# Two transformer blocks on one core: TensorE takes over the pooling's means, VectorE the queries' rotation, scores move to other PSUM banks, and the mLSTM's queries and keys are worked in twelve blocks of 128 features

## The reference, cut to what matters

```python
def mlstm_mixer(u, ...):                       # first block, layer 1
    qk, v, o_pre, gates = split(u, [1536, 2304, 3072])
    qk = silu(causal_dwconv(qk, qk_conv_w))    # width 4, 1536 features
    q, k = split(qk, 2)                        # 4 heads of 192 features
    h = mlstm_chunkwise(q, k, v, log_i, log_f)
    h = (h - mean) * rsqrt(var + eps) * head_norm_g
    return sigmoid(o_pre) * h

def mixer_sublayer(h, ...):                    # second block
    u_pool, u_conv, c_q, c_kv, k_r, g_logits = split(h @ w_in, ...)
    gates = sigmoid(g_logits + b_gate)         # 3 x 1024 features
    y_pool = pool_mixer(u_pool) @ pool_proj    # 4 groups of 128 features
    y_conv = conv_module(u_conv) @ conv_proj   # a * sigmoid(gate), 31 taps,
                                               # layer norm, silu
    y_mla = mla(c_q, c_kv, k_r, ...) @ mla_proj  # 8 heads, 64 + 32 features,
                                               # the 32 are rotated
    return (gates[0]*y_pool + gates[1]*y_conv + gates[2]*y_mla) @ w_out

def pool_mixer(u, w_grp, scale):               # group g: window 2, 4, 8, 16
    mixed = mean of the last min(t + 1, window) tokens - u
    return (mixed @ w_grp[g]) * scale
```

## Time and profile before

| what | us |
|---|---|
| median of 3 runs (lowest, highest) | 1609.09 (1609.03, 1609.48) |
| the profiled execution's own time | 1608.99 |
| its span, from the first to the last instruction | 1607.2 |
| TensorE busy in the span | 1543.8 (96%) |
| VectorE busy | 1138.4 (71%) |
| ScalarE busy | 897.7 (56%) |
| GpSimd busy | 101.8 (6%) |
| mLSTM: first query pair to the end of the last | 721.5 to 783.3 |
| second block: end of the latents to the start of `mla_proj_2` | 1046 to 1217 |

### The profile page before, as it was taken

How to read it: one execution, slowest core, us unless ns; L and a number is a source line. 1 busy time by engine, 2 the same in 40 slices (tenths; PEclk the granted TensorE clock), 3 DMA queues, 4 the chain that set the end, 5 groups by cost and what they waited for, 6 DMA issues and landing times.

```text
span 1607.2 us, 22098 instructions
## 1 busy us (share of the span) xinstructions
PE 1543.8 (96%) x8926; PEld 1358.6 (85%) x8926; DVE 1138.4 (71%) x1628; ACT 897.7 (56%) x1356; POOL 101.8 (6%) x137
## 2 busy tenths in 40 slices
PE   7999999999999999999999999798999989999996
PEld 6888899888888888889978888797999778888885
DVE  5666666666667666655776566769867878989997
ACT  5455454455545555456545555444456657777774
POOL 0000000000000000001300000042002320000000
PEclk9999999999999999999999999899999999999998
DMA  9655454555555555343455554335334659999992
GB/s 359 211 191 197 159 196 162 195 218 197 186 183 198 196 183 191 138 148 101 160 207 222 189 197 162 133 125 210 131 106 164 234 210 350 354 347 345 359 368 103
DMA packets 48059, 332.99 MB, mean 207 GB/s; under 512 B 5712, under 2 KB 5840, under 8 KB 10192
## 3 DMA queue, kind: packets, MB, share of 16 engines
q1 hardware_dynamic: 46496, 321.43, 55.0%
q0 software_dynamic: 1456, 10.09, 1.6%
HBM read 330.45 MB, written 1.05 MB: 206 GB/s over the span
## 4 chain that ended last, share of the span: by engine, by line
PE 83%; DVE 10%; ACT 3%; POOL 1%; issue 1%; DMA 0%; SPq 0%; DVEq 0%; ACTq 0%; POOLq 0%
PE psw L505 54%; PE psy L505 28%; DVE wlo L1650 4%; DVE kT L2037 2%; PE psw L508 1%; ACT whi L1147 1%; POOL ar L2434 1%; DVE xs L1659 0%; DMA raw<-in_ws 0%; ACT xs L1147 0%; ACT ar L1147 0%; DVE x L1733 0%; POOL rstd L2354 0%; DVE gsel L2227 0%; DVE x L1746 0%
## 5 line engine op out<-in xcount | busy, mean ns | idle before, releaser
L1650 DVE TENSOR_TENSOR wlo<-raw,whi 128x1024 fp32r<-128x1024 f32 (+2 forms) x552 | 640.5, 1206 | 192.2 <-ACT whi L1147 186.7
L505 PE MATMUL psw<-xs,whi 128*128 128x512 f32 (+3 forms) x2544 | 687.3, 345 | 18.5 <-DVE wlo L1650 8.5
L1147 ACT ACTIVATE whi<-raw 128x1024 fp32r<-128x1024 f32 (+2 forms) x552 | 540.0, 1031 | 150.2 <-PE psy L505 107.0
L505 PE MATMUL psw<-xs,wlo 128*128 128x256 f32 (+2 forms) x1928 | 516.3, 282 | 2.1 <-DVE xs L1659 2.1
L505 PEld LDWEIGHTS psw<-xs,whi 128*128 128x128 f32 (+2 forms) x2544 | 427.4, 187 | 68.8 <-DVE wlo L1650 8.5
L505 PEld LDWEIGHTS psw<-xs,wlo 128*128 128x128 f32 (+2 forms) x1928 | 362.9, 188 | 17.4 <-issue 2.6
L505 PE MATMUL psw<-whi,xs 128*128 128x512 f32 (+1 forms) x704 | 178.9, 365 | 6.3 <-DVE xs L1659 5.1
L505 PE MATMUL psy<-whi,hhi 128*128 128x512 f32 x472 | 158.0, 390 | 0.0
L505 PE MATMUL psy<-whi,hlo 128*128 128x512 f32 x472 | 157.8, 389 | 0.0
L505 PE MATMUL psy<-wlo,hhi 128*128 128x512 f32 x472 | 157.7, 389 | 0.0
L505 PEld LDWEIGHTS psw<-whi,xs 128*128 128x128 f32 x704 | 126.0, 190 | 27.6 <-issue 2.6
(11 more groups left out here) (303 smaller groups left out, 1624.2 us busy)
## 6 DMA issues: line engine op xcount, KB each, us to landing
raw<-in_ws SPq DMA_DIRECT2D x252, 1024.0 KB, 4.8
ar<-in_ws SPq DMA_DIRECT2D x32, 1024.0 KB, 6.5
raw<-in_ws SPq DMA_DIRECT2D x17, 768.0 KB, 4.3
gb<-in_ln POOLq DMA_DIRECT2D x8, 1024.0 KB, 6.1
raw<-in_ws SPq DMA_DIRECT2D x4, 672.0 KB, 3.9
ar<-in_memT SPq DMA_DIRECT2D x2, 1024.0 KB, 13.7
ar<-in_xT SPq DMA_DIRECT2D x2, 512.0 KB, 5.4
raw<-in_ws SPq DMA_DIRECT2D x2, 512.0 KB, 6.3
```

Of the source, the lines that this page charges most:

```text
L505: return e.matmul(o, l, rr, start=start, stop=stop)
L1147: return e.activation(o, i, ACT.Copy, **k)
L1650: e.tensor_tensor(wlo[i % NS][:, c0:c1], raw_t[slot[i]][:, c0:c1], whi[i % NS][:, c0:c1].bitcast(f32), ALU.subtract).then_inc(*made.up((i, ...
```

## The change

- **mLSTM.** Queries and keys in 12 blocks of 128 features: three tiles of 256 columns for each of the two parts. Heads of 192 features now cross blocks, so `attend` takes 128 + 64 rows. The work between the tiles is dealt anew on six entries; `attend(2)` joins `attend(3)`, and `states(2)` joins `states(3)`, in the output gate.
- **Pooling.** The inputs are made token by row, in two tiles of 4 x 512 columns and 48 matmuls of 512. The means are a product with a constant matrix (`means`, 0.79 MB, a new input, loaded on GpSimd's queue into a buffer that the gates use later): eight f32 matmuls, 1,536 columns in all, between the two `uq` tiles. GpSimd's sums go. The groups' products stand behind gate half 1, in two banks.
- **Order.** `glu(0)` comes before the latents' transposes, the pooling's inputs after `glu(1)`. One gate half moves from behind `rstd` to ahead of the mean. The convolution's taps are dealt anew.
- **Rotation.** VectorE rotates the queries in six operations on 128x256; ScalarE spreads the keys.
- **Attention.** The scores use `psy` banks 6 and 7. ScalarE copies the turned queries and keys out ahead of the exponentials.
- **End.** ScalarE rounds the convolution's result before the sigmoids of a gate, and prepares one more tile there.

```diff
...
-    for h in range(4):
+    for j in range(3):
         for part in range(2):
-            n = 768 * part + 192 * h
-            tiles.append(("w_in_mlstm", (0,), 0, 8, n, n + 192))
+            n = 768 * part + 256 * j
+            tiles.append(("w_in_mlstm", (0,), 0, 8, n, n + 256))
...
-    for j in range(2):
-        tiles.append(("w_in_2", (0,), 0, 8, 256 * j, 256 * j + 256))
     for j in range(2):
         for part in range(2):
             n = 512 + 512 * part + 256 * j
             tiles.append(("w_in_2", (0,), 0, 8, n, n + 256))
+    rows("w_in_2", (0,), 8, 0, 512, 4)
...
+        means = mg[:, 0:4 * 384].rearrange("p (g n) -> p g n", g=4)
...
                 def attend(h):
-                    q_, k_ = qk[h % 2]
+                    rows = [(192 * h, 192 * h + 128), (192 * h + 128, 192 * h + 192)] if h % 2 == 0 else [
+                        (192 * h, 192 * h + 64), (192 * h + 64, 192 * h + 192)]
                     b = bank("attend", h)
                     for part in range(2):
-                        need.wait_ge(*act.at("qk", h, part))
-                    for f in range(2):
-                        mm(b[:, 0:256], k_[:, f, 0:128], q_[:, f, :], f == 0, f == 1)
-                    for f in range(2):
-                        ins = mm(b[:, 256:384], k_[:, f, 128:256], q_[:, f, 128:256], f == 0, f == 1)
+                        need.wait_ge(*act.at("qk", (192 * h + 191) // 256, part))
+                    at = [(qk[r0 // 256 % 2], r0 // 128 % 2, r0 % 128, (r1 - 1) % 128 + 1) for r0, r1 in rows]
+                    for f, ((q_, k_), blk, p0, p1) in enumerate(at):
+                        mm(b[:, 0:256], k_[p0:p1, blk, 0:128], q_[p0:p1, blk, :], f == 0, f == 1)
+                    for f, ((q_, k_), blk, p0, p1) in enumerate(at):
+                        ins = mm(b[:, 256:384], k_[p0:p1, blk, 128:256], q_[p0:p1, blk, 128:256], f == 0, f == 1)
...
-                for h in range(4):
+                steps = [lambda: (turn(1, 0), weights(0)), lambda: (value(1, 0), turn(1, 1), weights(1)),
+                         lambda: (attend(0), value(1, 1), turn(1, 2)), lambda: (states(0), value(1, 2), turn(1, 3), weights(2)),
+                         lambda: (attend(1), value(1, 3), weights(3)), lambda: (states(1), finish(1))]
+                for j in range(3):
                     for part in range(2):
-                        pair(("head", h, part), Tile("w_in_mlstm", 768 * part + 192 * h), xhi, xlo, x_rows(4), m=96)
+                        pair(("head", j, part), Tile("w_in_mlstm", 768 * part + 256 * j), xhi, xlo, x_rows(4))
...
-                         {0: lambda: attend(3), 1: lambda: states(3)})
+                         {0: lambda: (attend(2), attend(3)), 1: lambda: (states(2), states(3))})
...
+            glu(0)
...
+            glu(1)
+            rows_p = [bank("pool", t) for t in range(2)]
             for j in range(2):
-                pair(("glu", 0, j), Tile("w_in_2", 512 + 256 * j), xhi, xlo, x_rows(6))
-                pair(("glu", 1, j), Tile("w_in_2", 1024 + 256 * j), xhi, xlo, x_rows(6))
+                w = Tile("w_in_2", 0)
+                for t in range(2):
+                    done = ([("bank", ("pool", t))] if j else []) + ([w.used()] if t else [])
+                    rows_of(w, t, xhi, xlo, w.k0, [(rows_p[t][:, :], 0, 512)], j == 0, j == 1, x_rows(6), [done] if done else ())
+
+            def pool_means():
+
+                for i in range(2):
+                    b = bank("pooled", i)
+                    need.wait_ge(*act.at("up", 1))
+                    need.wait_ge(*means_in.at("means"))
+                    for f in range(2):
+                        g, c = 2 * i + f, 256 * f
+                        mm(b[:, c:c + 256], up_[:, 0, 128 * g:128 * g + 128], means[:, g, 0:256], True, False)
+                        ins = mm(b[:, c + 128:c + 256], up_[:, 1, 128 * g:128 * g + 128], means[:, g, 256:384], False, True)
+                    ins.then_inc(*pe.up(("bank", ("pooled", i))))
+
+            def pool_groups():
+                for i in range(2):
+                    b = bank("poolw", i)
+                    need.wait_ge(*act.at("pooled", i))
+                    for f in range(2):
+                        g = 2 * i + f
+                        ins = mm(b[:, 256 * f:256 * f + 256], P("pool_w", 128 * g, 128 * g + 128), pooled[:, g, :], True, True)
+                    ins.then_inc(*pe.up(("bank", ("poolw", i))))
...
+                if i == 0:
+                    pool_means()
...
-            for _ in range(4):
+            for n in range(8):
                 gate_half()
-            for g in range(4):
-                b = bank("poolw", g)
-                need.wait_ge(*pool.at("pooled", g))
-                ins = mm(b[:, 0:256], P("pool_w", 128 * g, 128 * g + 128), pooled[g][:, 16:272], True, True)
-                ins.then_inc(*pe.up(("bank", ("poolw", g))))
-            for _ in range(4):
-                gate_half()
+                if n == 1:
+                    pool_groups()
...
-                b = bank("scores", h)
+                b = claim(6 + i, "scores", h)
...
+            gate_half()
...
-            gate_half()
...
+                steps = [lambda: (turn(1, 0), weights(0)), lambda: (turn(1, 1), weights(1)), lambda: turn(1, 2),
+                         lambda: (states(0), turn(1, 3), weights(2)), lambda: weights(3), lambda: (states(1), finish(1))]
...
+            glu(1)
+            w.tile()
+            w.tile()
+            for t in range(2):
+                from_bank(("pool", t), up_[:, t, :], flat, ("up", t))
...
+                if i == 0:
+                    for n in range(2):
+                        from_bank(("pooled", n), pooled[:, 2 * n:2 * n + 2, :], lambda b: blocks(b[:, :], 256), ("pooled", n))
...
+                need.wait_ge(*dve.at("kr", t))
+                copy(kf[:, t, :, 64:96], kr[:, t, :].unsqueeze(1).to_broadcast([128, 8, 32])).then_inc(*act.up(("kf", t)))
...
-                for back, stage in ((3, turn_p), (1, scores), (0, turn_qk)):
+                for back, stage in ((3, turn_p), (0, turn_qk), (1, scores)):
...
-            gate_half()
+            need.wait_ge(*act.at("ca", 3))
+            copy(mhi[:, 4:8, :], ca).then_inc(*act.up(("convhi",)))
+            w.ahead(3)
...
                 steps = [lambda: None, lambda: None, lambda: attend(0), lambda: states(0), lambda: (attend(1), scale(1)),
-                         lambda: (states(1), finish(1)), lambda: attend(2), lambda: states(2)]
-                for h in range(4):
+                         lambda: (states(1), finish(1))]
...
-                w.rows(4, {0: lambda: attend(3), 1: lambda: states(3)})
+                w.rows(4, {0: lambda: (attend(2), attend(3)), 1: lambda: (states(2), states(3))})
...
+
+            w.tile()
+            w.tile()
+            glu(0)
+            for i, nb, g in ((0, 3, "q_g"), (1, 2, "kv_g")):
...
+            w.tile()
+            conv_some(5)
+            w.tile()
+            conv_some(5)
+            glu(1)
+            conv_some(4)
             for i in range(2):
                 w.tile()
-                conv_some(6)
+                conv_some(7)
+            for i in range(2):
+                w.tile()
+                conv_some(5)
             w.rows(1)
-            conv_some(6)
+            conv_some(2)
+            need.wait_ge(*act.at("qf", 1, 1))
+            x1, x2 = qf[:, :, :, 64:80], qf[:, :, :, 80:96]
+            cb_ = cosA.unsqueeze(2).to_broadcast([128, 2, 8, 16])
+            sb_ = sinA.unsqueeze(2).to_broadcast([128, 2, 8, 16])
+            for i, (a, c) in enumerate(((x1, cb_), (x2, sb_), (x2, cb_), (x1, sb_))):
+                ins = e.tensor_tensor(roped[:, i, :, :, :], a, c, ALU.mult)
+            then(ins)
...
-            for _ in range(4):
+            for n in range(8):
                 gate_half()
-                conv_some(5)
-            for g in range(4):
...
-            conv_some(4)
+                if n == 1:
+                    for g in range(4):
+                        rest(mlo[:, g, :], place["poolw", g // 2][:, 256 * (g % 2):256 * (g % 2) + 256], mhi[:, g, :], ("poolhi", g // 2),
+                             P("pool_scale", g, g + 1)).then_inc(*dve.up(("poolT", g), *([took(("poolw", g // 2))] if g % 2 else [])))
+                conv_some(3)
...
-                    conv_some(3)
+                    conv_some(2)
...
                     scores(step - 1)
+                conv_some(4 if 0 < step < 9 else 5)
                 gate_half()
-                conv_some(4)
-            conv_some(1000)
...
+            gate_half()
+            conv_some(1000)
...
+            e.dma_start(means, A["means"][:, :].rearrange("p (g n) -> p g n", g=4)).then_inc(*means_in.up(("means",)))
...
-            then(e.memset(up_[:, :, 0:16], 0.0))
-            need.wait_ge(*act.at("up", 1))
-            for g in range(4):
-                src, lo = up_[:, g, :], 0
-                bufs = [wsum[:, g, :], wt2[:, g, :]]
```

(26 more changed lines are left out.)

168 lines of the change are left out of this document (71 added, 97 removed).

## The result

The kernel after takes 1582.99 us (median of 4 runs, 1581.49 to 1584.22), the kernel before on the same chip 1609.28 (1609.03 to 1610.63). The ratio is 0.9832, with an interval of 0.9820 to 0.9844 (the quotient of the two medians, 0.9837, lies inside it): 26.3 us less, where the forecast had 29.3.

What follows compares the result with a forecast made beforehand. TensorE was taken to bound the kernel, busy 96% of the span, but VectorE the second block. Terms summed to -29.3: span 1607.2 to 1577.9, with 1.8 around it and 0.1 for the median 1579.8, said as 1580; range 1576 to 1585.

Steps and rivals of the forecast that it cites:

- The pairs (-10.4): mLSTM: six pairs of 48 matmuls at 5.75 us replace eight at 5.61, saving 10.4 us.
- loading sets the pace, the rival: mLSTM pairs: weight loading sets the pace, so wider blocks cost what fewer save; 10.4 us lost, 1590; chance 0.03.
- at the same price, no gain: mLSTM's end: `attend(2)` and `states(2)` move behind the pairs at an unchanged price; no gain.
- The first wait (-3.3): mLSTM, second pair: spreading `weights` removes a bank wait of 1.6 us and 1.7 lost to the clock; -3.3.
- The end of the mLSTM (+0.4): mLSTM's end: heads 2 and 3 reach GpSimd together, so the heads' transposes wait; +0.4 us.
- the rival of +3: mLSTM's end: GpSimd takes two heads in a row at the highest price; +3, 1583; counted within the forecast's 0.62.
- The second block, what goes (-10.1): Second block: `zc` ready early, no wait for `poolT`; 6.7 us idle, 2.2 of clock and 1.2 of waits go; -10.1.
- The attention (-8.2): Second block's attention: ScalarE copying first removes waits of 3.1 and twice 1.25 us and 2.6 of clock; -8.2.
- The means (+2.8): Second block, between `uq`'s tiles: the pooling means as f32 matmuls on TensorE add 2.8 us.
- the inputs by row (-0.6): Second block: pooling inputs made by row take 10.9 us for 11.5; -0.6.
- The end (0): End of the mixers: ScalarE's rounding first changes nothing; 0, at the best -1.3 us.
- The rival on the other side: Attention: small f32 products and short bank waits keep the clock low; up to 38 us more, 1618; chance 0.02.

Runs made afterwards that it cites:

- e3: Kernel after with only the order of `attend`'s four products changed, to 128, 64, 64, 128 rows: 1582.07 us, ratio 0.9827.
- e1: Kernel after with all four `weights` of the mLSTM back in step 0: 1585.44 us, ratio 0.9846.
- e5: Kernel after with one `weights` behind tile 2 of the values' rows, two behind tile 3, one in step 0: 1580.87 us, ratio 0.9817.
- e6: Kernel after with both the edit of e5 and the order of `attend`'s products from e3: 1578.50 us, ratio 0.9807.
- e8: Kernel before with one line moved, GpSimd's memset of `zc` ahead of its pooling sums: 1607.67 us, ratio 0.9984.
- e9: Kernel after with ScalarE's old attention order, exponentials ahead of the copy of the turned queries and keys: 1585.00 us, ratio 0.9842.
- e12: Kernel after with ScalarE's old order at the mixers' end, sigmoids ahead of the rounding, no tile prepared ahead: 1584.17 us, ratio 0.9835.
- e10: Kernel after with the attention's scores back on the banks handed out in turn: 1582.96 us, ratio 0.9827.
- e2: Kernel after with all exponentials of `weights` ahead of the first silu, two of the four `weights` in step 0: 1584.86 us, ratio 0.9844.
- e4: Kernel after with both the early `weights` of e2 and the order of `attend`'s products from e3: 1584.17 us, ratio 0.9838.
- e7: Kernel before with the mLSTM's part of the change alone: 1599.59 us, ratio 0.9935.
- e11: Kernel after with the rotation of the queries given back to GpSimd: 1580.17 us, ratio 0.9818.

## Why the prediction was right, and where it was off

The direction, the place and most of the size were right: 26.3 us of 29.3. A gave 4.6 us less than forecast and C 1.1 more, and B came out 0.7 shorter, which isn't the change's; that the whole is off by only 3 is in part luck. To see which terms failed I take all the work in A and in C by its starts in TensorE's timeline, each piece from its start to the next one's. By the forecast's own steps:

- **The pairs (-10.4).** Right, -10.8. A pair of 128 columns takes 5.86 us (721.74 to 727.60), and the six 35.1 without the waits for silu; the eight of before, at 5.73 where nothing disturbed them, 45.9. The forecast had both prices 0.1 too low (5.75 and 5.61), as it took too much off for the attention product between two pairs (1.42 us for 1.23); the two errors nearly cancel. That loading sets the pace, the rival, is out.
- **`attend`, "at the same price, no gain".** This is the step that failed most: the four take 7.6 us for 5.1, so +2.5 where the forecast had 0. It counted records and columns and took the earlier trace rows for the price, though the split of the contraction changed from 96 + 96 to 128 + 64 rows. e3 showed that the changes between them cost part of it: halving them gave 0.7 back.
- **The first wait (-3.3).** The wait and its clock went, but they were worth 2.3 and not 3.3. The forecast took 1.6 us of idle time from the earlier trace rows, which are waits of PEld, the weight loading. TensorE's own timeline of before has one wait of 1.00, in the row below. The low clock behind it cost 1.3 us by the length of the next pair, where the forecast had 1.7.

```profile
729.95 1.36 PE L505 MATMUL psw<-ar 4*128 4x256 f32 x4 [1.00 <-ACT ar L1147]
```

- **`weights` spread over the steps.** It was costed by its banks alone, with 0.1 for silu. Its price on ScalarE, six table loads, came back as two new waits for silu of 0.51 and 0.53 us, which make two pairs 1.35 longer (the third, of 0.30, was there before as 0.22). And the small products around it took 0.7 more. Most of that are the transposes and the memory's products, 9.4 us for 8.9 in A; in e1 and e5, where the `weights` stand together, they take 8.9 again. e5 took 1.6 us of A away.
- **The end of the mLSTM (+0.4).** Cheaper, 0: GpSimd was done at 797.0 and VectorE's products at 800.9, ahead of the transposes at 802.25; the rival of +3 is out.
- With these the 4.6 us missing in A are accounted for: 2.5 `attend`, 1.25 silu, 1.0 the first wait, 0.7 the small products, less 0.4 each for the pairs and the end. e6 gets 2.6 of them back.
- **The second block, what goes (-10.1).** From the start of C to the first transposes of the attention TensorE took 94.8 us before (1045.76 to 1140.53) and 87.0 after (1036.65 to 1123.62): -7.8, where the forecast with the means and the inputs had -7.9. There is no wait for `zc` or `poolT`. But the first reason given, that `zc` is there sooner, is worth 1.9 us by itself (e8); the count of VectorE's queue behind it carried the term. VectorE took `poolT` at 1095.03, after waiting 0.46 us for ScalarE's part of it, and about 5.4 us before gate half 4 began at 1100.5.
- **The attention (-8.2).** From there to `mla_proj_2` it is 76.4 us before and 67.0 after: -9.4, so the 1.1 us that C gained over the sum lie here. The three waits of before and the low clock behind them cost about 9.1 us by the lengths of the products there, not 8.2. No wait is left and no stretch below 1.00. ScalarE's order, undone alone, is about half of it (e9), and for two of the three waits it isn't shown to be the cause.
- **The means (+2.8), the inputs by row (-0.6).** The means took 2.5 us from start to start, the inputs 10.91 (1062.13 to 1073.04): right. A step took 4.91 us and not 5.1.
- **The end (0).** Right as a sum, 46.46 to 46.27. But it needs ScalarE's new order there: without the earlier rounding and the tile prepared with it, it is 2.7 us longer (e12).
- **The clock.** The rival on the other side is out: 1.00 over all the attention, with the scores' small f32 products between the halves. The Trainium skill's case (TensorE: Matmul & The Clock Gate, section on PSUM-queue cycling) was not met here.

## What to carry to other kernels

Before spreading small work over a loop, count its price on every engine, not only the resource that it frees: an exponential between two silus is two table loads, and a step has room for as many banks as are empty by then. An early start helps an engine only if its queue can use it, so look for the point where the queue is full; ahead of that point idle time costs nothing. When a wait is to be priced, read it in the row of the engine that does the work: TensorE's own wait was 1.00 us where its weight loading showed 1.6. And compare traces by stretches between common starts: e10 and e12 were "the same" by their whole time and 1.9 and 2.7 us slower where they differed.

## What the runs showed of the hardware

- **Table loads.** A load took 1.28 us each time. The Trainium skill (ScalarE: Activation LUTs, section What ACT_TABLE_LOAD costs) gives the same 1.28 and adds 1.38 us of drain to each. The trace doesn't show the drain: the copy in front of the load ends at 738.98, the load at 739.00 ends at 740.28, and the exponential starts at 740.30.
- **A change of rows.** When weights of 64 rows follow weights of 128, or the other way, behind a product of 256 columns, PEld has a gap of 0.33 us, in after and in e3; behind one of 128 columns no gap shows. The same gap stands in after where a pair on 128 rows follows `weights` on 4 rows and 256 columns (765.34). 96 rows behind 128 showed no such gap in the kernel before. The Trainium skill (TensorEngine Tiling (Array Packing), section Key Properties) says that a change of the tiling mode drains TensorE, without a price. If 128 to 64 rows is such a change, the trace agrees behind 256 columns and shows nothing of it behind 128. The row of PEld at 765.34:

```profile
765.34 0.30 PEld L506 LDWEIGHTS psw<-xs,whi 128*128 128x128 f32 x2 [0.33 <-issue]
```

- **A wait and its clock.** The same code and the same wait of 1.0 us behind the first pair had two prices. Before: a granted clock of 0.66 for 5.05 us, then 1.00. e8: 0.56 for 5.0 us and 0.74 for 4.8 more, a mix of the 1.2 and 2.4 GHz levels. By the lengths of the products there, wait and clock cost 2.3 us before and 3.9 in e8, and that makes the 1.6 us by which A of e8 is longer. So A of e1, e2 and e4, with waits of 2.8 us, is uncertain by as much, while A of the kernels without that wait repeats within 0.05 us (after, e7, e9 to e12). The stretches of e8:

```profile
728.20:733.20 5.00, 5.00 (x20) 4.16 (x21) 2.32 (x6) 4.97 (x12) 2.59 (x8) 0.56 0.44 157
733.20:738.00 4.80, 4.80 (x33) 4.80 (x32) 1.83 (x2) 1.29 (x2) 0.00 (x0) 0.74 0.24 55
```

- **GpSimd beside VectorE.** Taps of 0.40 us took 0.56 (e8) and 0.63 (e11), subtractions of a tile 1.44 in place of 1.18 (e11: two in 2.88). GpSimd pays too: an addition of 0.52 us took 1.33 beside such a subtraction (e11, at 1089.02).
